# Hybrid mixer and top-4-of-32 MoE layer: turning the expert activations on ScalarE and VectorE instead of on TensorE

## The chip, the core and the metric

The kernel runs on one core of a Trainium2 chip. The metric is the device time of one execution in microseconds (us), as the median of repeated runs. A profile of one execution stands beside it: it has the start and the length of every instruction on TensorE (PE, with its weight loads as PEld), VectorE (DVE), ScalarE (ACT), GpSimd (POOL) and SyncE (SP), and of the DMA packets.

## What is computed

One layer over 1024 latent tokens of width 1024 (with 256 context tokens): a mixer of a recurrence (RG-LRU) and gated linear attention, layer norm, then a mixture of experts. Each token goes to 4 of 32 experts. The part that the change touches is the expert block:

```
def expert_block(args):
    tok, e = args
    xb = xt[tok]                                    # up to 128 rows of one expert
    gate = jnp.minimum(xb @ w_gate[e] + b_gate[e], SWIGLU_LIMIT)
    up = jnp.clip(xb @ w_up[e] + b_up[e], -SWIGLU_LIMIT, SWIGLU_LIMIT)
    act = (up + 1.0) * gate * jax.nn.sigmoid(SWIGLU_ALPHA * gate)
    return act @ w_down[e] + b_down[e]
```

All three weight matrices are 1024 x 1024 in fp32. The product with `w_down` needs `act` with its features on the partitions, while `gate` and `up` leave it with its rows on the partitions. So every block of `act` has to be turned between the two.

## The kernel before

After the mixer (to about 700 us) the kernel builds a table of jobs on the chip. A job is up to 128 rows of one expert, and its **kind** is 4 (full: 128 rows), 3 (96 rows), 2 (64) or 1 (32). A remainder of an expert is a job of kind 1 to 3, and its full jobs follow it. Jobs of kind 2 put the two halves of the 1024 output columns on the two halves of the partitions, jobs of kind 1 the four quarters on the four quarters, and kind 3 does both one after the other (`JOB_KINDS`). All engines walk the same table in loops of their own; branches (`by_kind`) pick the code for a kind.

TensorE's loop for job u works in this order: the first half of `gate_up` of job u (k = 0 to 3 of the eight 128-row blocks of `w_gate` and `w_up`), `turn` of job u-1 (transposes of `ub` by the identity into `psT`), the second half of `gate_up` of job u, `down` of job u-1. I write G(u) and D(u) for `gate_up` and `down` of job u.

VectorE's loop for job u: copy half of the turned activations of job u-1 from PSUM to `aT` (L1792), `turn_rows_in` for job u+1 (L1618, after G(u)), `swiglu` of job u (L1626 to L1641: bias of gate and of up, clamp, two products), `weigh` of job u-1 (L1607, L1612, after D(u-1)). The next `gate_up` waits for `gu_free`, which L1629 raises. ScalarE copies the other half of `aT` (L1217) and does the sigmoid (L1220). GpSimd gathers rows, spreads biases and scatters results.

Weights come in pieces of 1 MB into twelve fixed places: eight for gate and up (two for each pair of k), four for down. SP issues a piece of the next expert (L503, L531) when TensorE has raised `gu_used` or `dn_used` for that place, which it does in the last job of an expert. In `gate_up` the rise comes with the last sweep over k:

```
if k % 2 and sweep == sweeps[-1]:
    mm.then_inc(gu_used, 1)
```

Kind 3 has two sweeps, "half" and then "quarter", and each call of `gate_up` does both over its own range k0 to k1.

In the profiled execution there are 49 jobs. Jobs 2, 7, 11, 16, 21, 23, 30 and 31 are of kind 3; jobs 3, 5, 10, 12, 17, 18, 24, 32, 43 and 45 of kind 2; jobs 8, 15, 20, 27, 33, 35, 39 and 47 of kind 1; the other 23 of kind 4. Every job of kind 3 is the only one of its expert.

Of the kernel before, what the change touches and what calls it, by code (L numbers as in the profile page):

```python
# [13 lines left out]
ALU = mybir.AluOpType  # L14
# [23 lines left out]
def layer(nc, x, c, ctx, c_ctx, w_ada, b_ada, w_in, conv_w, conv_b, lru_wa, lru_ba, lru_wx, lru_bx,  # L38
# [41 lines left out]
    with ctxs:  # L80
# [159 lines left out]
        aT = reg(o, KD, P); o += 1024  # L240
        yb = reg(o, D); o += 1024
# [71 lines left out]
        act_turned, aT_act, aT_dve = sem("act_turned"), sem("aT_act"), sem("aT_dve")  # L313
# [98 lines left out]
        def natural(ap):  # L412
            return ap.rearrange("p (b a i) -> p b a i", a=4, b=KD)

# [10 lines left out]
        def _(sp):  # L425
# [193 lines left out]
        def down(pe, kind, u, order_):  # L619
            pe.wait_ge(aT_act, u + 1)  # L620
            pe.wait_ge(aT_dve, u + 1)
            pe.wait_ge(y_biased, u + 1)
            sweeps = {4: ("full",), 3: ("half", "quarter"), 2: ("half",), 1: ("quarter",)}[kind]
            for sweep in sweeps:
                for k in range(KD):
# [9 lines left out]
                    if sweep == "half":  # L635
                        for j in range(2):
                            mm = pe.matmul(ps[6][HT * j:HT * j + HT, :], aT[:, k % 4, HT * (k // 4):HT * (k // 4) + HT],  # L637
                                           w[:, j * BANK:(j + 1) * BANK],
                                           start=(k == 0), stop=(k == KD - 1), skip_group_check=True)
                    if sweep == "quarter":  # L640
                        for j in range(4):
                            mm = pe.matmul(ps[7][QR * j:QR * j + QR, 0:QW], aT[:, 4 + k % 2, QR * (k // 2):QR * (k // 2) + QR],  # L642
                                           w[:, j * QW:(j + 1) * QW],
                                           start=(k == 0), stop=(k == KD - 1), skip_group_check=True)
# [26 lines left out]

        def turn(pe, src, n, first=0):
            for k in range(first, n):
                mm = pe.transpose(psT[:, k * P:(k + 1) * P], src[:, k * P:(k + 1) * P], ident[:, :])  # L674
            return mm

        @block.tensor
        def _(pe):
# [297 lines left out]
            pe.nop().then_inc(act_turned, 1)  # L976
# [9 lines left out]
            with pe.Fori(0, OUTER) as o4:  # L986
                with pe.If(typ_of(pe, typ_p) + typ_of(pe, typ_c) > 0):
                    with pe.Fori(0, INNER) as i4:
                        u = o4 * INNER + i4 + 1
                        with pe.If(typ_of(pe, typ_p) + typ_of(pe, typ_c) > 0):  # L990
                            t, on_ = typ_of(pe, typ_c), ord_of(pe, ord_c, wait_c)
                            by_kind(pe, t, lambda kind: gate_up(pe, kind, u, on_, 0, KD // 2))
                            tp, op_ = typ_of(pe, typ_p), ord_of(pe, ord_p, wait_p)
                            with pe.If(tp > 0):
                                pe.wait_ge(act_ready, u + 1)
                                by_kind(pe, tp, lambda kind: turn(pe, ub, JOB_KINDS[kind][2] // P, JOB_KINDS[kind][1] // P).then_inc(act_turned, 1))
                                pe.nop()
                            by_kind(pe, t, lambda kind: gate_up(pe, kind, u, on_, KD // 2, KD))
# [24 lines left out]
        def _(act):  # L1023
# [182 lines left out]
            act.nop().then_inc(aT_act, 1)  # L1206
# [52 lines left out]
        def _(dve):  # L1259
# [360 lines left out]
            def swiglu(u, kind):  # L1620
# [7 lines left out]
                for p0, p1, c, b, n in parts:  # L1628
# [12 lines left out]
                dve.scalar_tensor_tensor(out=ub[:, w], in0=sg[:, w], scalar=s7, in1=ub[:, w], op0=ALU.min,  # L1641
                                         op1=ALU.mult).then_inc(act_ready, 1)
# [63 lines left out]
            dve.nop().then_inc(aT_dve, 1)  # L1706
# [307 lines left out]
```

## Time and profile before

| | us |
|---|---|
| time, median of 3 runs | 2355.92 (2355.53 to 2364.61) |
| span of the profiled execution, first to last instruction | 2352.5 |
| PE busy | 2191.9 (93% of the span) |
| DVE busy | 1021.4 |
| ACT busy | 466.7 |
| POOL busy | 444.8 |
| read from HBM | 480.51 MB, 218 GB/s over the span |

The profile has no other time for the profiled execution than its span; the median lies 3.4 us above it. A row of a group of instructions gives engine, line, operation, tiles, shapes, count, busy time and mean length, then the idle time of the engine just before it and what ended that. A row of the timeline gives the start, the length of a run of alike instructions, and in brackets the idle time before it. One fp32 matmul shows as two records, one transpose as one.

### The profile page before, as it was taken

What the parts mean: (1) busy time and instruction counts of PE and PEld (TensorE: products, weight loads), DVE (VectorE), ACT (ScalarE), POOL (GpSimd) and SP (SyncE); (2) the same over time, 40 slices, a digit from 0 to 9 for tenths busy, and PEclk for the clock granted to TensorE, in tenths of its full rate; (3) what the DMA queues carried; (4) which work ended last, traced back from release to release, by engine and by line L of the source; (5) the groups of instructions that cost most, each with busy time, mean ns of one, the idle gap of its engine ahead of it and who ended that gap; (6) DMA issues with size and microseconds to landing.
All of it is one profiled execution on the core that took longest, in us unless ns stands there. A gap on an engine that the chain in (4) does not pass through costs nothing.

```text
span 2352.5 us, 33568 instructions
## 1 busy us (share of the span) xinstructions
PE 2191.9 (93%) x9959; PEld 1018.7 (43%) x9960; DVE 1021.4 (43%) x1587; ACT 466.7 (20%) x624; POOL 444.8 (19%) x417
## 2 busy tenths in 40 slices
PE   5889999879968999999999899999999999999995
PEld 3444444464544444443443344444443444444442
DVE  3575754465775243444334243423253333222235
ACT  2334434331220111111111111111111111111113
POOL 0010100001231122222222132312213222122110
PEclk9989999889968999999999999999999999999997
DMA  8222221012252776889489999747899558897644
GB/s 330 84 67 69 89 72 36 1 73 84 89 214 91 240 296 213 298 291 400 135 284 399 355 354 407 256 158 246 297 376 349 204 174 297 291 324 240 214 128 154
DMA packets 168969, 510.55 MB, mean 217 GB/s; under 512 B 16434, under 2 KB 51002, under 8 KB 167770
## 3 DMA queue, kind: packets, MB, share of 16 engines
q1 hardware_dynamic: 153802, 474.25, 53.9%
q0 software_dynamic: 15120, 35.67, 6.9%
q8 instruction: 30, 0.49, 0.1%
q14 instruction: 17, 0.14, 0.0%
HBM read 480.51 MB, written 31.46 MB: 218 GB/s over the span
## 4 chain that ended last, share of the span: by engine, by line
PE 85%; DVE 7%; DMA 3%; issue 2%; ACT 1%; SPq 1%; DVEq 0%; POOL 0%; POOLq 0%
PE psall L605 27%; PE psall L633 14%; PE psall L609 10%; PE psall L776 10%; PE psall L637 5%; PE psall L614 4%; PE psall L764 3%; PE psall L887 2%; PE psall L881 2%; DMA arena<-in_w_down_dram 2%; PE psall L674 1%; PE psall L743 1%; DMA arena<-in_x_dram 1%; PE psall L642 1%; DVE arena L1423 1%
## 5 line engine op out<-in xcount | busy, mean ns | idle before, releaser
L605 PE MATMUL psall<-arena 128*128 128x512 f32 x1472 | 645.7, 597 | 27.5 <-issue 22.3
L605 PEld LDWEIGHTS psall<-arena 128*128 128x128 f32 x1472 | 278.6, 191 | 373.0 <-issue 373.0
L633 PE MATMUL psall<-arena 128*128 128x512 f32 x736 | 323.5, 598 | 4.8 <-DVE arena L1792 3.2
L609 PE MATMUL psall<-arena 128*64 128x512 f32 x1152 | 258.5, 600 | 8.9 <-DVE arena L1629 3.7
L1618 DVE STREAM_TRANSPOSE arena<-arena 128x1024 f32<-128x1024 f32 x49 | 61.0, 1246 | 453.6 <-PE psall L605 276.5
L776 PE MATMUL psall<-arena 128*128 128x512 f32 (+1 forms) x608 | 246.5, 563 | 0.7 <-ACT arena L1037 0.7
L633 PEld LDWEIGHTS psall<-arena 128*128 128x128 f32 x736 | 139.5, 191 | 183.3 <-issue 183.3
L1217 ACT COPY arena<-psall 128x512 f32<-128x512 f32 x49 | 28.7, 586 | 792.1 <-PE psall L674 792.1
L1792 DVE COPY arena<-psall 128x512 f32<-128x512 f32 x49 | 33.9, 692 | 323.3 <-PE psall L674 323.1
L776 PEld LDWEIGHTS psall<-arena 128*128 128x128 f32 x608 | 116.5, 192 | 120.6 <-issue 116.3
L1220 ACT ACTIVATE arena<-arena 128x1024 f32<-128x1024 f32 x49 | 51.8, 1057 | 582.5 <-DVE arena L1626 582.5
L1607 DVE TENSOR_TENSOR arena<-psall,arena 32x256 f32<-32x256 f32 (+2 forms) x123 | 79.8, 649 | 191.8 <-PE psall L633 147.7
L1893 POOL DMA_INDIRECT arena<-h_rows,lruw x144 | 147.0, 1021 | 83.0 <-POOL lruw L1886 39.4
L609 PEld LDWEIGHTS psall<-arena 128*64 128x64 f32 x1152 | 83.7, 138 | 167.4 <-issue 167.4
L637 PE MATMUL psall<-arena 128*64 128x512 f32 x576 | 128.6, 595 | 8.0 <-DMA arena<-in_w_down_dram 7.4
L1886 POOL COPY lruw<-arena 128x4 int32 (+1 forms) x48 | 9.2, 191 | 631.0 <-DVE arena L1618 602.5
L614 PE MATMUL psall<-arena 128*32 128x256 f32 x2048 | 117.3, 381 | 2.5 <-issue 1.4
L1907 POOL DMA_INDIRECT stream_rows<-arena,lruw x57 | 92.9, 1630 | 93.9 <-DMA stream_rows<-arena,lruw 42.2
L1612 DVE SCALAR_TENSOR_TENSOR arena<-arena,lruw,adarow 32x256 f32<-32x256 f32 (+2 forms) x123 | 90.9, 739 | 6.7
L614 PEld LDWEIGHTS psall<-arena 128*32 128x32 f32 x2048 | 64.1, 110 | 60.3 <-issue 22.9
L1626 DVE TENSOR_TENSOR arena<-psall,arena 32x256 f32<-32x256 f32 (+2 forms) x123 | 78.0, 634 | 14.0 <-PE psall L605 13.0
L637 PEld LDWEIGHTS psall<-arena 128*64 128x64 f32 x576 | 41.6, 137 | 91.6 <-issue 91.6
(319 smaller groups left out, 2098.6 us busy)
## 6 DMA issues: line engine op xcount, KB each, us to landing
arena<-in_w_gate_dram SPq DMA_DIRECT2D x128, 1024.0 KB, 6.5
arena<-in_w_up_dram SPq DMA_DIRECT2D x128, 1024.0 KB, 8.6
arena<-in_w_down_dram SPq DMA_DIRECT2D x128, 1024.0 KB, 8.9
arena<-in_w_ada_dram SPq DMA_DIRECT2D x16, 1024.0 KB, 5.3
arena<-in_w_ada_dram SPq DMA_DIRECT2D x4, 2048.0 KB, 14.2
arena<-in_w_in_dram SPq DMA_DIRECT2D x16, 512.0 KB, 4.0
arena<-in_x_dram SPq DMA_DIRECT2D x2, 2048.0 KB, 28.4
arena<-in_w_out_dram SPq DMA_DIRECT2D x1, 4096.0 KB, 14.1
```

What stands on the lines that cost most here:

```text
L605: mm = pe.matmul(ps[2 * g + s], xT[:, k, :], w[:, s * BANK:(s + 1) * BANK], start=(k == 0), stop=(k == KD - 1))
L609: mm = pe.matmul(ps[2 * g][HT * j:HT * j + HT, :], xT[:, k, 0:HT], w[:, j * BANK:(j + 1) * BANK], start=(k == 0), stop=(k == KD - 1), skip ...
L614: mm = pe.matmul(ps[2 * g + 1][QR * j:QR * j + QR, 0:QW], xT[:, k, r], w[:, j * QW:(j + 1) * QW], start=(k == 0), stop=(k == KD - 1), skip ...
L633: mm = pe.matmul(ps[6 + s], aT[:, k, :], w[:, s * BANK:(s + 1) * BANK], start=(k == 0), stop=(k == KD - 1))
L637: mm = pe.matmul(ps[6][HT * j:HT * j + HT, :], aT[:, k % 4, HT * (k // 4):HT * (k // 4) + HT], w[:, j * BANK:(j + 1) * BANK], start=(k == ...
L764: mm = pe.matmul(ps[i % JB][:, :], uT[:, k, j * P:(j + 1) * P], wv[:, k, :], start=(k == 0), stop=(k == KD - 1))
L776: mm = pe.matmul(ps[i % JB][0:w, 0:seg[1] - seg[0]], wring[n % WRING][:, k, 0:w], uT[:, k, seg[0]:seg[1]], start=(k == 0), stop=(k == KD - 1))
L1607: mm = dve.tensor_tensor(yb[p0:p1, c:c + n], psY[p0:p1, c:c + n], ebias[p0:p1, 2, b:b + n], ALU.add)
L1612: mm = dve.scalar_tensor_tensor(out=yb[p0:p1, c:c + n], in0=yb[p0:p1, c:c + n], scalar=(wcolq if c else wcol)[p0:p1], in1=adarow[p0:p1, 3, ...
L1626: mm = dve.tensor_tensor(gb[p0:p1, c:c + n], psG[p0:p1, c:c + n], ebias[p0:p1, 0, b:b + n], ALU.add)
L1893: pool.indirect_dma_start(out=xg[:, CW * t:CW * (t + 1)], out_offset=None, in_=h2_dram.rearrange("a (j n) -> (a j) n", n=CW), in_offset=ba ...
L1907: return pool.indirect_dma_start(out=to, out_offset=bass.IndirectOffsetOnAxis(ap=index, axis=0), in_=yb[:, cols], in_offset=None, bounds_c ...
```

## The change

TensorE no longer turns the activations. `gate_up` of a job now runs over all eight k in one call, and `down` of the job before follows at once. The last product of `swiglu` leaves the activations in `ub` (kinds 4, 2, and the first part of kind 3) or, reordered, in a new tile `act_rows` (kind 1 and the second part of kind 3). ScalarE then copies quarters (32 partitions x 256 columns) from `ub` to other partitions of `act_rows`: 16 copies for kind 4, 8 for kinds 3 and 2, none for kind 1. Each reads every eighth column and writes without gaps. VectorE turns 32 x 32 blocks from `act_rows` to `aT` in one instruction, and `down` waits for that. Since the features now lie on the partitions in another order (eight neighbours on one partition), `w_down` is loaded so that partition p gets rows 8p to 8p+7; a piece is two of these eight rows (8 KB in one run on each partition) where it was two separate rows of 4 KB.

```
             def dn_pieces(e, u):
                 for q in range(DNP):
                     sp.wait_ge(dn_used, DNP * u + (q + 1))
-                    w_v = w_down[0].rearrange("e (q c p) n -> e q p c n", c=2, p=P)[:, q]
+                    w_v = w_down[0].rearrange("e (p k) n -> e p k n", k=KD)[:, :, 2 * q:2 * q + 2]
...
         def down(pe, kind, u, order_):
-            pe.wait_ge(aT_act, u + 1)
-            pe.wait_ge(aT_dve, u + 1)
+            pe.wait_ge(aT_ready, u + 1)
...
-                            by_kind(pe, t, lambda kind: gate_up(pe, kind, u, on_, 0, KD // 2))
+                            by_kind(pe, t, lambda kind: gate_up(pe, kind, u, on_, 0, KD))
                             tp, op_ = typ_of(pe, typ_p), ord_of(pe, ord_p, wait_p)
-                            with pe.If(tp > 0):
-                                pe.wait_ge(act_ready, u + 1)
-                                by_kind(pe, tp, lambda kind: turn(pe, ub, JOB_KINDS[kind][2] // P, JOB_KINDS[kind][1] // P).then_inc(act_turned, 1))
-                                pe.nop()
-                            by_kind(pe, t, lambda kind: gate_up(pe, kind, u, on_, KD // 2, KD))
...
+            def spread(u, kind):
+                act.wait_ge(act_ready, u + 1)
+                if kind == 1:
+                    act.nop().then_inc(act_spread, 1)
+                    return
+                if kind == 4:
+                    moves = [(t, a, QW * a) for t in range(4) for a in range(4)]
+                else:
+                    moves = [(t, 2 * j + h, QW * h) for t in range(2) for j in range(2) for h in range(2)]
+                for t, a, c in moves:
+                    of = QR * t + (0 if kind == 4 else HT * (a // 2))
+                    mm = act.copy(by_block(act_rows[QR * a:QR * a + QR, QW * t:QW * t + QW]),
+                                  by_feature(ub[of:of + QR, c:c + QW]))
+                mm.then_inc(act_spread, 1)
...
-                            act.wait_ge(act_turned, u + 1)
-                            act.copy(aT[:, 0:4].rearrange("p k n -> p (k n)"), ps[4]).then_inc(aT_act, 1)
+                            by_kind(act, typ_of(act, typ_p), lambda kind: spread(u, kind))
...
+            def turn_act(kind):
+                lo, hi = JOB_KINDS[kind][1] // QW, JOB_KINDS[kind][2] // QW
+                dve.transpose(aT.rearrange("p b (t s) -> p t b s", t=4)[:, lo:hi],
+                              act_rows.rearrange("p (t b i) -> p t b i", t=4, b=KD)[:, lo:hi]).then_inc(aT_ready, 1)
...
-                            dve.wait_ge(act_turned, u + 1)
-                            dve.tensor_copy(aT[:, 4:8].rearrange("p k n -> p (k n)"), ps[5]).then_inc(aT_dve, 1)
+                            dve.wait_ge(act_spread, u)
+                            by_kind(dve, tp, turn_act)
```

TensorE, body of the job loop, the branches for kinds 4 and 3. Before, `gate_up` stands in two halves with the transposes (L674) between them:

```order
L605 MATMUL psall<-arena 128x512 x16
L650 UNCONDITIONAL_BRANCH
L591 ISA
L609 MATMUL psall<-arena 64x512 x16
L614 MATMUL psall<-arena 32x256 x32
...
L674 MATMUL psall<-ident,arena 128x128 x8
L650 UNCONDITIONAL_BRANCH
L674 MATMUL psall<-ident,arena 128x128 x6
...
L609 MATMUL psall<-arena 64x512 x16
L614 MATMUL psall<-arena 32x256 x32
```

After, L612, L616 and L621 are the same matmuls:

```order
L612 MATMUL psall<-arena 128x512 x32
L655 UNCONDITIONAL_BRANCH
L598 ISA
L616 MATMUL psall<-arena 64x512 x32
L621 MATMUL psall<-arena 32x256 x64
```

The transposes are gone, and in kind 3 all 64x512 matmuls (k = 0 to 7) now stand ahead of all 32x256 ones, where they took turns in two halves.

ScalarE, body of the job loop. Before, one copy from PSUM and the sigmoid:

```order
L1217 ACT_TABLE_LOAD
L1217 COPY arena<-psall 128x512
L1215 UNCONDITIONAL_BRANCH
L1218 COMPARE_AND_BRANCH
L1219 ISA
L1220 ACT_TABLE_LOAD
L1220 ACTIVATE arena<-arena 128x1024
```

After, the branches for kinds 4, 3 and 2, then the sigmoid (L1229):

```order
L1212 COPY arena<-arena 32x256 x16
L655 UNCONDITIONAL_BRANCH
L1202 ISA
L1212 ACT_TABLE_LOAD
L1212 COPY arena<-arena 32x256 x8
...
L1229 ACT_TABLE_LOAD
L1229 ACTIVATE arena<-arena 128x1024
```

One copy per job became 16 or 8, between the act of a job and the VectorE instruction that turns it.

## Rows read from the trace of the kernel before

**Rows 1.** The page's chain that ended last, share of the span by engine.

```profile
PE 85%; DVE 7%; DMA 3%; issue 2%; ACT 1%; SPq 1%; DVEq 0%; POOL 0%; POOLq 0%
```

**Rows 2.** Groups by shape: the transposes, and VectorE's block transpose of the next rows.

```profile
L674 PE MATMUL psall<-ident,arena 128*128 128x128 f32 x288 | 41.8, 282 | 2.5 <-DVE arena L1641 2.5
...
L1618 DVE STREAM_TRANSPOSE arena<-arena 128x1024 f32<-128x1024 f32 x49 | 61.0, 1246 | 453.6 <-PE psall L605 276.5 <-PE psall L614 99.2 <-PE psall L609 67.4
```

**Rows 3.** Timeline of TensorE, jobs 19 to 21: start, us, engine, line, [idle before].

```profile
1348.69 7.09 PE L637 MATMUL psall<-arena 128*64 128x512 f32 x32
1355.71 3.66 PE L614 MATMUL psall<-arena 128*32 128x256 f32 x64
1359.30 1.09 PE L674 MATMUL psall<-ident,arena 128*128 128x128 f32 x8
1360.32 3.66 PE L614 MATMUL psall<-arena 128*32 128x256 f32 x64
```

**Rows 4.** Timeline of VectorE in the same place.

```profile
1348.92 1.25 DVE L1618 STREAM_TRANSPOSE arena<-arena 128x1024 f32<-128x1024 f32 x1 [13.16 <-PE psall L605]
...
1354.65 1.23 DVE L1641 SCALAR_TENSOR_TENSOR arena<-arena 128x1024 f32<-128x1024 f32 x1
```

**Rows 5.** Timeline of TensorE, job 34 (full) between two quarter jobs.

```profile
1829.77 3.66 PE L642 MATMUL psall<-arena 128*32 128x256 f32 x64
1833.93 3.66 PE L614 MATMUL psall<-arena 128*32 128x256 f32 x64 [0.50 <-DVE arena L1629]
1837.53 1.09 PE L674 MATMUL psall<-ident,arena 128*128 128x128 f32 x8
1838.55 3.66 PE L614 MATMUL psall<-arena 128*32 128x256 f32 x64
1842.46 13.97 PE L633 MATMUL psall<-arena 128*128 128x512 f32 x32 [0.25 <-DVE arena L1792]
```

**Rows 6.** Groups by shape of ScalarE: immediate operands, strided and unstrided output, two partition starts.

```profile
L1062 ACT ACTIVATE arena<-arena 128x1280 f32<-128x1280 f32 x4 | 5.0, 1254 | 0.0
L1060 ACT ACTIVATE arena<-arena 128x1024 f32<-128x1024 f32 x4 | 4.2, 1040 | 0.0
L1109 ACT ACTIVATE arena<-psall,par 128x512 f32<-128x512 f32 x8 | 9.8, 1230 | 42.4 <-PE psall L776 42.4
L1109 ACT ACTIVATE arena<-psall,par 128x256 f32<-128x256 f32 x4 | 2.2, 562 | 4.9 <-PE psall L776 4.9
28.88 1.18 ACT L1031 COPY adarow<-psall 2x512 f32<-2x512 f32 x2 [17.67 <-PE psall L689]
```

**Rows 7.** Timeline of TensorE: a full job's half after a wait of 3.45 us.

```profile
1407.40 15.67 PE L605 MATMUL psall<-arena 128*128 128x512 f32 x32 [3.45 <-DVE arena L1629]
```

**Rows 8.** Timelines at the last job: VectorE's last product and TensorE.

```profile
2293.57 1.23 DVE L1641 SCALAR_TENSOR_TENSOR arena<-arena 128x1024 f32<-128x1024 f32 x1
...
2299.99 16.56 PE L633 MATMUL psall<-arena 128*128 128x512 f32 x32 [2.94 <-DVE arena L1792]
```

**Rows 9.** Timelines at job 30 (kind 3): TensorE, and SP's first issues.

```profile
1685.42 7.09 PE L609 MATMUL psall<-arena 128*64 128x512 f32 x32
...
1692.44 3.66 PE L614 MATMUL psall<-arena 128*32 128x256 f32 x64
...
1694.15 0.40 SPq L503 DMA_DIRECT2D arena<-in_w_gate_dram  x1
```

**Rows 10.** Stretches: us, busy of PE, PEld, DVE, ACT, POOL, clock, DMA share, GB/s.

```profile
18.00:34.00 16.00, 8.15 (x49) 2.68 (x42) 1.38 (x2) 1.15 (x2) 0.00 (x0) 0.83 1.01 413
1212.00:1320.00 108.00, 96.29 (x661) 38.78 (x652) 45.62 (x76) 16.83 (x16) 29.31 (x29) 0.97 1.02 389
1685.00:1802.00 117.00, 110.61 (x859) 45.84 (x858) 56.36 (x90) 16.83 (x16) 28.62 (x28) 1.00 0.95 356
```

**Rows 11.** Timeline of TensorE: the last waits for weights in the two stretches.

```profile
1318.72 1.94 PE L637 MATMUL psall<-arena 128*64 128x512 f32 x8 [1.87 <-DMA arena<-in_w_down_dram]
...
1800.02 1.94 PE L637 MATMUL psall<-arena 128*64 128x512 f32 x8 [1.03 <-DMA arena<-in_w_down_dram]
```

More of the change, by code:

```diff
@@ L240, in layer @@
         aT = reg(o, KD, P); o += 1024
+        act_rows = reg(O_X1 + 19456, D)
         yb = reg(o, D); o += 1024
@@ L312, in layer @@
             sem("g_biased"), sem("sg_ready"), sem("u_clipped"), sem("ug_ready"), sem("act_ready"))
-        act_turned, aT_act, aT_dve = sem("act_turned"), sem("aT_act"), sem("aT_dve")
+        act_spread, aT_ready = sem("act_spread"), sem("aT_ready")
         y_dve, y_stored, yq_stored, yb_free = sem("y_dve"), sem("y_stored"), sem("yq_stored"), sem("yb_free")
@@ L413, in natural, with by_feature, by_block @@
             return ap.rearrange("p (b a i) -> p b a i", a=4, b=KD)
+        def by_feature(ap):
+            return ap.rearrange("p (i b) -> p b i", b=KD)
+        def by_block(ap):
+            return ap.rearrange("p (b i) -> p b i", b=KD)
         def o_at(T, h):
@@ L636, in down @@
                         for j in range(2):
-                            mm = pe.matmul(ps[6][HT * j:HT * j + HT, :], aT[:, k % 4, HT * (k // 4):HT * (k // 4) + HT],
-                                           w[:, j * BANK:(j + 1) * BANK],
+                            mm = pe.matmul(ps[6][HT * j:HT * j + HT, :], aT[:, k, 0:HT], w[:, j * BANK:(j + 1) * BANK],
                                            start=(k == 0), stop=(k == KD - 1), skip_group_check=True)
@@ L641, in down @@
                         for j in range(4):
-                            mm = pe.matmul(ps[7][QR * j:QR * j + QR, 0:QW], aT[:, 4 + k % 2, QR * (k // 2):QR * (k // 2) + QR],
+                            mm = pe.matmul(ps[7][QR * j:QR * j + QR, 0:QW], aT[:, k, HT:HT + QR],
                                            w[:, j * QW:(j + 1) * QW],
@@ L670, in ord_of @@
             return eng.snap(bounded, min_val=16, max_val=16 * NE)
[L672 to L675, printed above, removed]
         @block.tensor
@@ L974, in job_lists @@
                 mm.then_inc(half_mm, 1)
-            pe.nop().then_inc(act_turned, 1)
             pe.wait_ge(tab_ready, 16)
@@ L1215, in _ @@
                         with act.If(typ_of(act, typ_p) > 0):
-                            act.wait_ge(act_turned, u + 1)
-                            act.copy(aT[:, 0:4].rearrange("p k n -> p (k n)"), ps[4]).then_inc(aT_act, 1)
+                            by_kind(act, typ_of(act, typ_p), lambda kind: spread(u, kind))
+                            act.nop()
                         with act.If(typ_of(act, typ_c) > 0):
@@ L1640, in swiglu @@
                 dve.wait_ge(ug_ready, u + 1)
-                dve.scalar_tensor_tensor(out=ub[:, w], in0=sg[:, w], scalar=s7, in1=ub[:, w], op0=ALU.min,
-                                         op1=ALU.mult).then_inc(act_ready, 1)
+                for p0, p1, c, b, n in parts:
+                    if p0 == 0:
+                        w = slice(c, c + n)
+                        out, in0, in1 = ub[:, w], sg[:, w], ub[:, w]
+                        if c:
+                            out, in0, in1 = by_block(act_rows[:, w]), by_feature(in0), by_feature(in1)
+                        mm = dve.scalar_tensor_tensor(out=out, in0=in0, scalar=s7, in1=in1, op0=ALU.min, op1=ALU.mult)
+                mm.then_inc(act_ready, 1)
+            def turn_act(kind):
+                lo, hi = JOB_KINDS[kind][1] // QW, JOB_KINDS[kind][2] // QW
+                dve.transpose(aT.rearrange("p b (t s) -> p t b s", t=4)[:, lo:hi],
+                              act_rows.rearrange("p (t b i) -> p t b i", t=4, b=KD)[:, lo:hi]).then_inc(aT_ready, 1)
             first_ranks(NT - 1, NT + 1)
@@ L1705, in _ @@
             turn_rows_in()
-            dve.nop().then_inc(aT_dve, 1)
+            dve.nop().then_inc(aT_ready, 1)
             dve.nop().then_inc(act_ready, 1)
```

2 lines of the change are left out of this document (1 added, 1 removed).

## The prediction

> **What bounds the kernel now.** I read the chain of waits first: 85% of the span hangs on PE [rows 1], so time goes away only where PE has less to do or waits less. Then the groups by shape, for the price of what goes and of its nearest kin [rows 2, 6], and the timeline of PE through the jobs [rows 3, 5]. There the matmuls of one job follow those of the next without a gap almost everywhere. The transposes (L674) lie in this row of work, so they cost their own time, and nothing waits for them but VectorE's and ScalarE's copies. Two stretches are different: from 1212 to 1320 us and from 1685 to 1802 us the DMA engines are busy at a share of 1.02 and 0.95 [rows 10], and each ends with PE waiting for weights [rows 11]. In these the bytes set the time, and not PE.
>
> **What goes from PE.** 288 transposes [rows 2]. Eight of them take from 1359.30 to 1360.32, 1.02 us until the next matmul starts [rows 3]; next to full jobs it is 0.88, and the sum over the 48 groups that lie between matmuls is 34.7 us. The last group is no part of it: there PE is idle anyway. VectorE's copy of 128x512 goes too, but it lies beside PE's work. First term: **-34.7 us**.
>
> **What the new chain costs.** From the end of G(u) to D(u) PE has D(u-1) and G(u+1) to do. In that time VectorE must turn the next rows and do the five steps of `swiglu`, ScalarE must make its copies, VectorE must turn blocks. At a full job the last product ends 7.2 us after G's end (1348.69 to 1354.65 + 1.23) [rows 3, 4]. The block transpose of a full job has the shape of L1618: 1.25 us [rows 2]; I add 0.1 us at either side of ScalarE's part. The copies are the unknown. On ScalarE 256 more columns cost 1254 - 1040 = 214 ns, so 256 columns with immediate operands cost 1040 - 3 x 214 = 398 ns [rows 6]. That is without a stride. L1109 with a gap-free output takes 562 ns for 256 columns, hence 348 + 214; into strided columns it takes 1230 ns for 512, hence 348 + 882, or 1.72 ns a column where 0.84 is normal. Our copies read with a stride of eight columns. No row shows a strided read from SBUF on this engine, so the bounds are 398 ns and 184 + 441 = 625 ns. I take 625, since L1109 is the only row of this engine with a stride. Do successive copies overlap? The two L1031 copies start on different partitions, and take 1.18 us for 2 x 575 ns: no overlap, 0.03 us between [rows 6]. Each copy here goes to another quarter than the one before. So a full job's 16 copies cost 16 x 0.655 = 10.5 us, or 16 x 0.43 = 6.9 at the lower bound, and aT is ready 7.2 + 0.1 + 10.5 + 0.1 + 1.25 = 19.1 us after G(u)'s end, or 15.5.
>
> Where is PE there sooner? Among full jobs, PE is away 42 us, and with a quarter job behind and a full one before, 21; all covered. The tight ones are these. Job 34 (full) stands between two quarter jobs: G(35) starts 4.16 us after G(34)'s end and takes 2 x 3.6, so PE is free at 11.4 [rows 5]. It waits 7.7 where 0.25 stands now, and after such a wait it restarts slowly: 3.45 us of idleness came before a half that took 15.67 us [rows 7] where 13.97 is usual [rows 5], 1.7 more. Together +9.2. Jobs 19 and 46 (half before, quarter behind): PE is free at 7.0 + 3.6 + 3.6 = 14.2 [rows 3], waits 4.9 and restarts slowly: 2 x 6.6 = +13.2. Job 9 (quarter before, half behind): free at 18.0, +1.1. Job 48 is the last, nothing covers it: its product ends at 2294.80, aT at 2306.7, against a start of D at 2299.99 [rows 8]: +6.8. Second term: 9.2 + 13.2 + 1.1 + 6.8 = **+30.3 us**. With the lower bound it is 5.6 + 2.6 + 0 + 3.2 = +11.4.
>
> The steps of narrow jobs have half the copies (5.2 us) or none. A job of kind 3 has its last product 12.3 us after G's end and would be ready at about 19; PE comes at 21 or later.
>
> **What the weights cost.** In kind 3 the old order did the half sweep over k = 0 to 3, then the quarter sweep over them, and released four places after 7.02 + 3.66 us: SP's first issue comes 8.7 us after G(30)'s start [rows 9]. Now the half sweep runs over all eight k (14.0 us) before the first quarter matmul, so the first release comes at 14.0 + 1.8 = 15.9 us. Where the DMA engines have nothing left to do at that time, 7.2 us are lost to them. That is so at job 30, since its four places were empty until then. The chain of bytes from there to 1800.02 is 36 pieces. It starts 7.2 us later, gets back some 1 us of its own gaps and, by the packets of 8 KB, 12 down pieces x 0.08 = 1.0 us (413 GB/s in a stretch of 8 KB packets [rows 10] against 400 in the middle of the first stretch), and has another gap of 0.4 at job 31: +5.7 us. The four groups of transposes in it (3.2 us) bring nothing. So this stretch is 8.9 us worse than the first term says. In the first stretch pieces queue at job 16 until about the new release; its chain stays whole, gains 1.2, and 2.9 us of transposes bring nothing: +1.7. Behind jobs 7 and 11 a narrow job follows, and the down pieces queue behind eight pieces of gate and up: 15.9 + 12 x 2.8 = 49.5 us for the last, where D(7) wants it at 21.4 + 14.0 + 7.3 + 3 x 1.8 = 48.1. I take +3.5 for both. Third term: 8.9 + 1.7 + 3.5 = **+14.1 us**.
>
> **The sum.** -34.7 + 30.3 + 14.1 = +9.7 us. The span goes from 2352.5 to 2362.2, and with the 3.4 us by which the median lies above the span, the time is **2366 us**. Its own range is 2355 to 2377: the slow restarts are uncertain by 4 us, the weights by 6.
>
> A page that speaks against this change: the Trainium skill, "SBUF — State Buffer", section "Door 1: The DMA port swizzle", says that accesses which cross to a new 16-byte line each time pay a penalty, so that fp32 may stride over four elements for free. Our copies stride over eight. By that rule the upper price stands; without it the sum would be 18.9 us lower. L1109's row agrees for a write; none here shows the read.
>
> **Rivals.** *Cheap copies.* A read with a stride is free, as nothing shows that it isn't. The second term is 11.4: -34.7 + 11.4 + 14.1 = -9.2, so 2347 us, range 2338 to 2353. For it: in ScalarE's strided row only the output is strided. Against: the output's store and the input's read go to the same memory. *Down pieces that come slowly.* The new view of `w_down` takes 8 KB from each 32 KB, over the whole 4 MB, where a piece was 1 MB in one run. If such a piece took twice its time (2.7 us more), the 12 pieces of each stretch bound by bytes would add 32 us, and 12 more in the jobs 7 and 11: 2366 + 76 = 2442 us. It decides from about 0.5 us a piece, which would bring 12 + 3 us. Against: the first loads take 8 KB from every 24 KB, and run at 413 GB/s [rows 10]. The Trainium skill, "DMA: Bandwidth & Descriptors", section "Latency and other measured facts", has large powers of two as a row pitch slow, but starts at 512 KiB with 207 GB/s of 214; by it 32 KB costs nothing. *The release doesn't matter.* If the queue at job 30 hides the late release, the third term is 5 and the time 2357, or with cheap copies 2338.
>
> **Chances.** The forecast 0.48, cheap copies 0.32, slow down pieces 0.08, no effect of the release 0.12 (half of it with cheap copies). A measurement of this kernel can tell 0.5% (11.8 us: below 2344.1, above 2367.7) from no change. Of the forecast 0.22 lies above 2367.7, the rest within; of cheap copies 0.15 lies below 2344.1; of the last rival 0.06 does. So faster 0.21, same 0.49, slower 0.30. The range from 2338 to 2380 leaves out the slow pieces and the tails, some 0.15.
>
> **What would show it.** The changed kernel's profile should have 23 x 16 + 18 x 8 = 512 copies of 32x256 on ScalarE at a mean of 625 ns (398 if a strided read is free); no idle time before D but at jobs 34, 19, 46, 9 and 48, put down to VectorE's block transpose; SP's first issue in job 30 some 16 us after its G starts; waits for `w_up` and `w_down` in jobs 32 and 33 that sum to some 12 us where 4 stand now; and packets of 8 KB for `w_down` at twice the time of those of 4 KB. The forecast is wrong if the copies overlap after all, if PE doesn't slow down after waits of 5 us, or if the first sweep of kind 3 isn't what holds the places.

## The result, and the profile after

The changed kernel takes 2373.7 us (median of its runs, 2371.5 to 2376.75), the kernel before beside it 2359.0. The ratio is 1.0061, with a 95% interval of 1.004 to 1.0081. That is 14 us slower, 9 to 19 by the interval; the forecast was 10 us slower and a time of 2366 us. The span is 2369.8 us, 17.3 longer. The page of the kernel after has busy times and the chain of waits [rows 1]:

```profile
PE 2163.5 (91%) x9671; PEld 1001.1 (42%) x9672; DVE 1040.2 (44%) x1595; ACT 762.5 (32%) x1079; POOL 445.8 (19%) x417
...
PE 79%; DVE 8%; DMA 5%; ACT 3%; issue 2%; SPq 2%; DVEq 0%; POOL 0%; ACTq 0%; POOLq 0%
```

PE is busy for 28.4 us less (2191.9 before), and the span still grew: its share of the chain fell from 85 to 79%, ScalarE and the DMAs got two points each, and VectorE and SP one each. The groups by shape say what the new operations cost [rows 2, 6]:

```profile
L1212 ACT COPY arena<-arena 32x256 f32<-32x256 f32 x512 | 334.4, 653 | 99.2 <-DVE arena L1656 86.9 <-issue 6.8
...
L1661 DVE STREAM_TRANSPOSE arena<-arena 128x1024 f32<-128x1024 f32 x23 | 28.6, 1245 | 109.0 <-ACT arena L1212 108.8 <-issue 0.2
```

A copy takes 653 ns (forecast 625), and nearly all the idle time of VectorE ahead of its block transpose ends with the last copy. The timeline of PE shows where it waits for this transpose, in jobs 9, 19, 34, 46 and 48 [rows 5, 7, 8]; line L639 is L633 of before:

```profile
1065.41 14.00 PE L639 MATMUL psall<-arena 128*128 128x512 f32 x32 [1.62 <-DVE arena L1661]
...
1369.98 15.48 PE L639 MATMUL psall<-arena 128*128 128x512 f32 x32 [5.48 <-DVE arena L1661]
...
1852.60 16.51 PE L639 MATMUL psall<-arena 128*128 128x512 f32 x32 [5.18 <-DVE arena L1661]
...
2255.42 16.48 PE L639 MATMUL psall<-arena 128*128 128x512 f32 x32 [4.96 <-DVE arena L1661]
...
2317.29 16.27 PE L639 MATMUL psall<-arena 128*128 128x512 f32 x32 [14.32 <-DVE arena L1661]
```

These are the five places that the prediction named, and no other `down` waits for the block transpose: the view of waits has `PE psall L639 <- DVE arena L1661` five times, 31.6 us in all. The same timeline shows two losses of another kind, ahead of the first `down` and inside `down` of job 7:

```profile
787.82 13.97 PE L639 MATMUL psall<-arena 128*128 128x512 f32 x32 [2.98 <-issue]
...
1001.64 1.94 PE L643 MATMUL psall<-arena 128*64 128x512 f32 x8 [1.10 <-DMA arena<-in_w_down_dram]
1004.26 1.94 PE L643 MATMUL psall<-arena 128*64 128x512 f32 x8 [0.68 <-DMA arena<-in_w_down_dram]
1008.65 1.94 PE L643 MATMUL psall<-arena 128*64 128x512 f32 x8 [2.46 <-DMA arena<-in_w_down_dram]
1011.87 1.94 PE L643 MATMUL psall<-arena 128*64 128x512 f32 x8 [1.28 <-DMA arena<-in_w_down_dram]
```

In SP's timeline the first issue of job 30 comes 15.6 us after G(30)'s start (1684.98 in PE's timeline), where it was 8.7 [rows 9]:

```profile
1700.58 0.41 SPq L510 DMA_DIRECT2D arena<-in_w_gate_dram  x1
```

To put the difference into places I take every start from the first `gate_up` (711.14 us before, 710.66 after), since the part ahead of it varies by some us between executions. From there to the end it is 1641.4 us before and 1659.1 after, 17.7 more. As in the forecast's sum, the transposes stand in the last row wherever they lay, also beside a named job; only the two stretches stand with what their transposes bring:

| place | forecast, us | measured, us |
|---|---|---|
| ahead of D(0): the wait of 2.98, and 0.7 before G(1) | 0 | +3.6 |
| jobs 7 and 11, `down` waits for its weights | +3.5 | +10.3 (6.2 and 4.0) |
| job 9 | +1.1 | +1.5 |
| jobs 19 and 46 | +13.2 | +14.6 (6.9 and 7.7) |
| job 34 | +9.2 | +10.4 |
| last job | +6.8 | +6.9 |
| first stretch bound by bytes (G(15) to G(19)) | -1.2 | -1.3 |
| second (G(30) to G(34)) | +5.7 | +4.0 |
| everything else, mainly transposes | -28.6 | -32.1 |

The figure of job 34 has a part that is no wait for the turn. G(35), which PE runs just before D(34), takes 2.9 us longer than before; it has four gaps of 0.3 us, put down to "issue", and slower matmuls around them:

```profile
1837.26 1.89 PE L621 MATMUL psall<-arena 128*32 128x256 f32 x26 [0.53 <-DVE arena L1638]
...
1841.65 5.77 PE L621 MATMUL psall<-arena 128*32 128x256 f32 x98 [0.34 <-issue]
```

It costs nothing here: D(34) waits for the turn anyway, and in the first experiment below, where G(35) is 2.0 us quicker, it waits 2.0 us longer. Some of the other kernels have this slow G(35) too (those with one transpose and with kind 3's order alone), others don't; its cause stays open.

### The profile page after: what moved, and what is told of

Same layout as the page of the kernel before. It is cut to its first block, busy times and chain, and to the rows that moved or that the text cites. A ratio compares the mean times of both kernels' runs of the same rounds, so it can differ in the third digit from the quotient of the medians.

```text
span 2369.8 us, 33439 instructions
## 1 busy us (share of the span) xinstructions
PE 2163.5 (91%) x9671; PEld 1001.1 (42%) x9672; DVE 1040.2 (44%) x1595; ACT 762.5 (32%) x1079; POOL 445.8 (19%) x417
## 4 chain that ended last, share of the span: by engine, by line
PE 79%; DVE 8%; DMA 5%; ACT 3%; issue 2%; SPq 2%; DVEq 0%; POOL 0%; ACTq 0%; POOLq 0%
PE psall L612 26%; PE psall L639 14%; PE psall L776 10%; PE psall L616 9%; DMA arena<-in_w_down_dram 4%; PE psall L643 3%; PE psall L621 3%; PE psall L764 3%; PE psall L887 2%; PE psall L881 2%; ACT arena L1212 2%; PE psall L743 1%; DMA arena<-in_x_dram 1%; PE psall L647 1%; DVE arena L1432 1%
## 5 line engine op out<-in xcount | busy, mean ns | idle before, releaser
L612 PE MATMUL psall<-arena 128*128 128x512 f32 x1472 | 641.7, 596 | 27.9 <-issue 23.5
L612 PEld LDWEIGHTS psall<-arena 128*128 128x128 f32 x1472 | 280.3, 191 | 383.6 <-issue 383.6
L1212 ACT COPY arena<-arena 32x256 f32<-32x256 f32 x512 | 334.4, 653 | 99.2 <-DVE arena L1656 86.9
L1229 ACT ACTIVATE arena<-arena 128x1024 f32<-128x1024 f32 x49 | 51.8, 1057 | 968.4 <-DVE arena L1635 876.8
L639 PE MATMUL psall<-arena 128*128 128x512 f32 x736 | 329.9, 607 | 35.1 <-DVE arena L1661 31.6
L616 PE MATMUL psall<-arena 128*64 128x512 f32 x1152 | 253.5, 597 | 9.8 <-DMA arena<-in_w_up_dram 4.5
L639 PEld LDWEIGHTS psall<-arena 128*128 128x128 f32 x736 | 141.9, 195 | 217.9 <-issue 183.6
L616 PEld LDWEIGHTS psall<-arena 128*64 128x64 f32 x1152 | 86.6, 137 | 173.1 <-issue 173.0
L643 PE MATMUL psall<-arena 128*64 128x512 f32 x576 | 131.1, 597 | 16.9 <-DMA arena<-in_w_down_dram 16.0
L621 PE MATMUL psall<-arena 128*32 128x256 f32 x2048 | 118.8, 383 | 10.6 <-DMA arena<-in_w_up_dram 4.6
L1661 DVE STREAM_TRANSPOSE arena<-arena 128x1024 f32<-128x1024 f32 (+3 forms) x49 | 47.2, 962 | 128.0 <-ACT arena L1212 120.5
L621 PEld LDWEIGHTS psall<-arena 128*32 128x32 f32 x2048 | 70.4, 110 | 63.0 <-issue 27.9
L1621 DVE SCALAR_TENSOR_TENSOR arena<-arena,lruw,adarow 32x256 f32<-32x256 f32 (+2 forms) x123 | 89.6, 728 | 6.7
## 6 DMA issues: line engine op xcount, KB each, us to landing
arena<-in_w_out_dram SPq DMA_DIRECT2D x1, 4096.0 KB, 13.9
```

The costliest lines, as they stand in the source:

```text
L612: mm = pe.matmul(ps[2 * g + s], xT[:, k, :], w[:, s * BANK:(s + 1) * BANK], start=(k == 0), stop=(k == KD - 1))
L616: mm = pe.matmul(ps[2 * g][HT * j:HT * j + HT, :], xT[:, k, 0:HT], w[:, j * BANK:(j + 1) * BANK], start=(k == 0), stop=(k == KD - 1), skip ...
L621: mm = pe.matmul(ps[2 * g + 1][QR * j:QR * j + QR, 0:QW], xT[:, k, r], w[:, j * QW:(j + 1) * QW], start=(k == 0), stop=(k == KD - 1), skip ...
L639: mm = pe.matmul(ps[6 + s], aT[:, k, :], w[:, s * BANK:(s + 1) * BANK], start=(k == 0), stop=(k == KD - 1))
L643: mm = pe.matmul(ps[6][HT * j:HT * j + HT, :], aT[:, k, 0:HT], w[:, j * BANK:(j + 1) * BANK], start=(k == 0), stop=(k == KD - 1), skip_gro ...
L1212: mm = act.copy(by_block(act_rows[QR * a:QR * a + QR, QW * t:QW * t + QW]), by_feature(ub[of:of + QR, c:c + QW]))
```

## Experiments

All figures "from the first `gate_up`" are of one profiled execution of each kernel, like those above. Between executions they vary: D(0) alone took 13.9 us to the next start in two kernels with the new order and 15.3 to 15.6 in the others. The ratios are to the kernel before, on the same chip.

**Kind 3 in two half sweeps.** The changed kernel, but `gate_up` of kind 3 again does both sweeps over k = 0 to 3 and then both over 4 to 7.

```
-            for sweep in sweeps:
+            cuts = (k0, (k0 + k1) // 2, k1) if kind == 3 and k1 - k0 == KD else (k0, k1)
+            for sweep, k0, k1 in [(s, a, b) for a, b in zip(cuts, cuts[1:]) for s in sweeps]:
                 for k in range(k0, k1):
```

> The changed kernel, but gate_up of a job of kind 3 does its two sweeps over k = 0 to 3 and then over k = 4 to 7, as before the change. Theory (late release of the weight places in kind 3 costs time): SP's first issue in a kind 3 job comes 9 us after its start and not 15.6; the waits for w_down in D(7) and D(11), 5.5 and 3.3 us, are gone; the stretch of jobs 30 to 33 gets 4 to 6 us shorter; in all 10 to 14 us less than the changed kernel's span of 2369.8, so 2356 to 2360. Rival (the new view of w_down makes its pieces come late): the waits stay, and the span is within 2 us of 2369.8.

Measured: 2359.05 us, ratio 1.0023 (1.0012 to 1.0033); from the first `gate_up` 13.0 us less than the changed kernel. SP's first issue in job 30 comes 8.7 us after its start again (15.6 in the changed kernel), D(11) has no wait for weights, and neither has D(7):

```profile
1007.13 7.09 PE L644 MATMUL psall<-arena 128*64 128x512 f32 x32 [0.23 <-issue]
```

So the order of the sweeps, and not the removal of the transposes or the new view, is what made the weights late. At job 34 nothing is gained: G(35) is 2.0 us quicker, and the wait grows by as much, from 5.2 to 7.2.

**That order alone, in the kernel before.** The transposes stay; only kind 3 runs over all eight k ahead of them.

```
-by_kind(pe, t, lambda kind: gate_up(pe, kind, u, on_, 0, KD // 2))
+by_kind(pe, t, lambda kind: gate_up(pe, kind, u, on_, 0, KD if kind == 3 else KD // 2))
...
-by_kind(pe, t, lambda kind: gate_up(pe, kind, u, on_, KD // 2, KD))
+by_kind(pe, t, lambda kind: gate_up(pe, kind, u, on_, KD // 2, KD) if kind != 3 else pe.nop())
```

> The kernel before, transposes and all, with one thing changed: in jobs of kind 3 gate_up runs over all eight k ahead of the transposes of the job before, so that the quarter sweep (and with it the release of the places of gate and up) comes after the whole half sweep. Its third effect: turned activations of the job before come 10.7 us later, for which PE waits nowhere. Theory (the late release costs time by itself): jobs 7 and 11 wait for down pieces, 5 to 9 us together, jobs 32 and 33 wait 5 us more, so 10 to 14 us more than before. Rival (in the changed kernel the weights come late for another reason): within 3 us of before.

Measured: 2371.66 us, ratio 1.0052 (1.0032 to 1.0072), 14.3 us more from the first `gate_up`. Of this 3.1 lie at job 7, 1.0 at job 11 and 5.2 in the second stretch up to G(35), and another 3.0 in G(35), which I had not expected. Nor had I expected what the edit does besides: the turned activations come later, and PE does wait for them, in `down` of jobs 1, 6, 10, 22, 29 and 30, for 0.9 to 1.5 us each:

```profile
1102.37 7.09 PE L637 MATMUL psall<-arena 128*64 128x512 f32 x32 [1.45 <-DVE arena L1792]
```

They add 3.2 us of the 14.3. So the late weights by themselves cost 9 us (12 with G(35)), and that the whole comes out near the 13.0 of the repair is partly chance. Jobs 7 and 11 show why the changed kernel loses more there. From the start of G(7) to that of G(9), which follows D(7), it is 56.0 us before and 54.1 with the two half sweeps, but 59.5 here and 60.1 in the changed kernel. From G(11) to G(13) the four are 55.8, 54.2, 57.8 and 58.1. So with the late release the end of `down` is set by its last piece of weights, and what the missing transposes save ahead of it only makes the wait longer.

**The new view of `w_down` undone.** The changed kernel with `w_down` loaded as before. Its rows then don't match the order of the features, so its output is not the reference's.

```
-w_v = w_down[0].rearrange("e (p k) n -> e p k n", k=KD)[:, :, 2 * q:2 * q + 2]
+w_v = w_down[0].rearrange("e (q c p) n -> e q p c n", c=2, p=P)[:, q]
```

> The changed kernel, but w_down is loaded by the old view (two separate rows of 4 KB on each partition); since the activations are in the new order, this kernel multiplies each activation with another row of w_down, at the same cost. Theory (release order): the same waits in D(7) and D(11), span within 2 us of 2369.8, at most 2 us more in the two stretches bound by bytes (12 pieces x 0.08 us each). Rival (the view is slow): the waits in D(7) and D(11) go, and 9 us or more are gained.

Measured: 2377.74 us, ratio 1.0091 (1.0075 to 1.0107), 6.9 us *more* than the changed kernel from the first `gate_up`. The rival of slow down pieces is out: without the new view nothing is gained, and the waits in D(7) are still there (5.1 us). But only a small part of the 6.9 us is shown to be the view's. In each of the two stretches bound by bytes it is 0.7 us, within what I had allowed. Another 2.5 us lie ahead of G(2), before and in D(0), and 2.3 in D(7), where matmuls run slowly behind a wait (16 of them take 3.65 us at the usual pace):

```profile
790.39 15.67 PE L639 MATMUL psall<-arena 128*128 128x512 f32 x32 [3.96 <-issue]
...
1013.71 6.63 PE L643 MATMUL psall<-arena 128*64 128x512 f32 x16 [3.23 <-DMA arena<-in_w_down_dram]
```

The loss ahead of G(2) is no sign of the view: five kernels below that have the new view lose 2.0 to 3.4 us in the same place. Of the last 0.8 us 0.7 are again slow matmuls, in D(19).

**Packed reads.** The changed kernel, but VectorE's last product writes its result by blocks (it reads and writes with a stride instead), so ScalarE's copies read runs of 32 columns. The number of copies stays.

```
-                        out, in0, in1 = ub[:, w], sg[:, w], ub[:, w]
-                        if c:
-                            out, in0, in1 = by_block(act_rows[:, w]), by_feature(in0), by_feature(in1)
+                        out, in0, in1 = by_block((act_rows if c else gb)[:, w]), by_feature(sg[:, w]), by_feature(ub[:, w])
...
-                                  by_feature(ub[of:of + QR, c:c + QW]))
+                                  by_block(gb[of:of + QR, 0:D if kind == 4 else BANK])[:, :, c // KD:(c + QW) // KD])
```

> The changed kernel, but VectorE's last product reads every eighth column and writes gb without gaps, by blocks, and ScalarE's copies read runs of 32 neighbouring columns. Theory (ScalarE's price is the strided read): a copy takes some 400 ns where it takes 653, 16 of them 6.9 us where they take 10.6; the product of a full job takes 2.2 us where it takes 1.23 (its 256-column form with a stride takes 669 ns, without 439), so aT comes 2.7 us sooner. Waits in D(34), D(19), D(46) fall from 5.2 to 2.5, the last job gains 2.7, some 13 us in all with restarts: span 2355 to 2360. Rival (the price is that of 32 partitions, or of changing them): 653 ns stays, and the span grows by some 4 us.

Measured: 2358.02 us, ratio 1.0012 (1.0001 to 1.0023), 13.1 us less from the first `gate_up`. The groups by shape of this kernel:

```profile
L1212 ACT COPY arena<-arena 32x256 f32<-32x256 f32 x512 | 205.9, 402 | 124.8 <-DVE arena L1654 119.2
...
L1654 DVE SCALAR_TENSOR_TENSOR arena<-arena 128x1024 f32<-128x1024 f32 x23 | 46.6, 2027 | 2.4
```

A copy costs 402 ns now, which is the prediction's lower bound of 398. So the stride is the difference between the bounds. VectorE pays 0.8 us for it once (2027 ns for 1225), ScalarE had paid 0.25 us sixteen times. PE's waits fall to 2.22 us at job 19, 2.07 at job 46 and 11.22 at job 48. At job 34 the wait is 5.08, since G(35) is not slow here and PE comes 3.0 us sooner.

**Both repairs.**

> Both edits, those of kind 3's sweeps and of the packed product. If the two terms are independent, the gains add: 2369.8 - 12 - 13 = 2345, some 7 us (0.3%) less than the kernel before at 2352.5. If either rival holds, 2357 to 2372.

Measured: 2346.38 us, ratio 0.9958 (0.9943 to 0.9974), 25.9 us less than the changed kernel from the first `gate_up`. The two effects add up, 13.0 + 13.1, and with them the change becomes faster than the kernel before, by 0.4%.

**Only one copy.** The changed kernel with `for t, a, c in moves[:1]:` in `spread`.

> The changed kernel with only the first of ScalarE's copies in every job (the other quarters of act_rows stay stale, so this output isn't the reference's): aT is ready 9.8 us sooner after the last product of a full job, 4.6 us sooner in kinds 2 and 3. Theory (the row of copies costs its own length wherever PE is there sooner): the idle time before down of jobs 34, 19, 46 and 9 (5.2 + 5.5 + 5.0 + 1.6 us) goes but for a rest at job 34, the 14.3 us before the last down become 4.5, and the slow matmuls behind these waits (2.5 us at job 34, 1.5 at 19 and 2.5 at 46) come at their usual pace. 16.5 + 9.8 + about 4 = 30 us less than the changed kernel from the first gate_up on, of it 3 to 5 us given back in waits for weights, so 25 to 28 less. Rival (PE's waits are set elsewhere, by the other work of VectorE): under 12 us less.

Measured: 2345.31 us, ratio 0.9942 (0.9922 to 0.9963), 27.4 us less than the changed kernel from the first `gate_up`. The sum fits, but one part doesn't: the last `down` still waits 7.9 us, not 4.5. VectorE's timeline at the last job shows why:

```profile
2283.76 1.23 DVE L1656 SCALAR_TENSOR_TENSOR arena<-arena 128x1024 f32<-128x1024 f32 x1
2285.35 0.15 DVE L1610 COPY lruw<-lruw 128x1 f32 x1 [0.36 <-issue]
2285.57 1.72 DVE L1616 TENSOR_TENSOR arena<-psall,arena 32x256 f32<-32x256 f32 x4
2287.40 1.95 DVE L1621 SCALAR_TENSOR_TENSOR arena<-arena,lruw,adarow 32x256 f32<-32x256 f32 x4
2289.38 1.25 DVE L1661 STREAM_TRANSPOSE arena<-arena 128x1024 f32<-128x1024 f32 x1
```

The block transpose follows without a gap on `weigh` of job 47 (L1610 to L1621, 4 us). So there is a second chain under the copies: once they take less than some 4.4 us, VectorE's own queue holds the transpose.

**One transpose a job.** The kernel before with the first block of `turn` alone; 239 of the 288 transposes are left out, and the output is not the reference's.

> The kernel before with one transpose in each job where it has 8, 6, 4 or 2 (the other blocks of psT stay stale, so this output isn't the reference's): 239 of the 288 transposes are gone, in the same order of work. Theory (PE's row of matmuls is the bound outside of the two stretches bound by bytes): 239 x 0.12 = 29 us less, of which 5 us are absorbed in the two stretches: 23 to 26 us less than before. Rival (it is absorbed in much more of the program): under 15 us less.

Measured: 2337.49 us, ratio 0.9903 (0.9886 to 0.992), which is 19 to 27 us; from the first `gate_up` only 16.7. Seven transposes of a full job bring 0.77 us, and all that are left out between matmuls 22.1 (34.7 - 12.6), not the 29 that I had multiplied out. So 5.4 us are given back: 2.6 in G(35), some 1.4 in the first stretch bound by bytes, 0.8 in a wait for weights at job 11 and the rest in small parts. The transposes lie on the path, and what is absorbed is about the 5 us that I expected.

**Copies shared with VectorE.** Both repairs, and VectorE makes every second copy right after its last product.

```
+                if kind == 1:
+                    dve.nop().then_inc(dve_spread, 1)
+                else:
+                    dve.wait_ge(act_ready, u + 2)
+                    move(dve, kind, 1).then_inc(dve_spread, 1)
...
                             dve.wait_ge(act_spread, u)
+                            dve.wait_ge(dve_spread, u)
```

> The kernel with both repairs (packed reads, two half sweeps in kind 3), in which VectorE makes every second copy, right after its last product, and ScalarE the others. A full job has 8 copies on each engine, 3.3 us on ScalarE where 6.6 stood. Theory (the chain from the last product to aT is what PE waits for, and VectorE is free then): 3.3 us less at job 34 and at job 48, 1.6 less at each of jobs 19 and 46, some 2 us of slow restarts less: 10 to 12 us less than with both repairs alone. Rival (the copies of the two engines hold each other up, or VectorE's copies push its later steps): no gain, or slower.

Measured: 2348.41 us, ratio 0.9952 (0.9936 to 0.9967); from the first `gate_up` 2.3 us more than with both repairs alone. The rival holds. ScalarE is done after 3.3 us, but VectorE isn't. Its timeline at job 19:

```profile
1347.74 2.07 DVE L1659 SCALAR_TENSOR_TENSOR arena<-arena 128x1024 f32<-128x1024 f32 x1
1349.85 4.37 DVE L430 COPY arena<-arena 32x256 f32<-32x256 f32 x8
1354.25 0.15 DVE L1613 COPY lruw<-lruw 128x1 f32 x1
1354.33 1.39 DVE L1621 TENSOR_TENSOR arena<-psall,arena 64x512 f32<-64x512 f32 x2
1355.84 1.51 DVE L1626 SCALAR_TENSOR_TENSOR arena<-arena,lruw,adarow 64x512 f32<-64x512 f32 x2
1357.75 1.25 DVE L1669 STREAM_TRANSPOSE arena<-arena 128x1024 f32<-128x1024 f32 x1 [0.40 <-issue]
```

2.0 us of the copies' 4.37 are one copy beside a broadcast of GpSimd (last section). Copies and `weigh` stand one after the other ahead of the transpose, and PE's wait at job 19 grew from 2.23 to 3.21 us. By the ratios, which overlap, this kernel and the one with both repairs are equal; the sharing gains nothing.

**Another order on VectorE.** Both repairs and shared copies, but in a job VectorE now does: last product, bias of the job before, 6 of the 16 copies, block transpose, and only then the scaling of the job before.

```
-                        with dve.If(tp > 0):
-                            dve.wait_ge(act_spread, u)
-                            dve.wait_ge(dve_spread, u)
-                            settle(dve)
-                            by_kind(dve, tp, turn_act)
...
                             by_kind(dve, tp, lambda kind: weigh(u, kind, orderp))
+                        with dve.If(typ_of(dve, typ_c) > 0):
+                            by_kind(dve, typ_of(dve, typ_c), lambda kind: spread_dve(u, kind))
+                            dve.wait_ge(act_spread, u + 1)
+                            dve.wait_ge(dve_spread, u + 1)
+                            by_kind(dve, typ_of(dve, typ_c), turn_act)
+                        with dve.If(tp > 0):
+                            by_kind(dve, tp, lambda kind: scale_out(u, kind))
```

> The kernel with both repairs, with VectorE's work of a job in another order: last product, bias of the job before (3 of its 4 us in shared and one_copy stood ahead of the turn), 6 of 16 copies (ScalarE makes the other 10), turn of the blocks, and only then the scaling of the job before. Theory (what holds the turn in shared and one_copy is VectorE's own queue: copies and weigh stand between the last product and the turn): at a full job with a quarter job before it, the turn starts 4.1 us after the last product instead of 6.6, so the stall before down of jobs 34 and 48 is 2.7 us shorter than with both repairs alone, and that of jobs 19 and 46 goes: 7 to 9 us less than with both repairs alone, 0.993 of the kernel before. Rival (something else than this queue holds the turn): the same as both repairs alone, 0.996.

Measured: 2332.67 us, ratio 0.9894 (0.9875 to 0.9912), 14.6 us less than with both repairs alone from the first `gate_up`. This is the fastest kernel here, 1.1% faster than before. PE's rows at jobs 34, 46 and 48:

```profile
1827.52 14.00 PE L652 MATMUL psall<-arena 128*128 128x512 f32 x32 [1.25 <-DVE arena L1674]
...
2222.90 14.00 PE L652 MATMUL psall<-arena 128*128 128x512 f32 x32 [0.28 <-DVE arena L1674]
...
2276.79 16.61 PE L652 MATMUL psall<-arena 128*128 128x512 f32 x32 [8.84 <-DVE arena L1674]
```

The waits fell by about what was expected (3.1, 1.8 and 2.4 us; the one at job 19, 2.2 us, is gone). The gain is larger than the 7 to 9 us because the matmuls at four places are no longer slow: D(19), D(34) and D(46) take 13.8 to 13.9 us to the next start, where they took 15.3 to 15.6, and G(22) takes 27.70 where it took 29.29, behind a wait that hardly changed (3.24 us for 3.34). These four bring 6.5 us, which I had left out of the sum. The kernel differs from the one with both repairs in two things, the order and who makes the copies; the kernel with shared copies has the second alone (8 of 16 on VectorE), and gained nothing.

## Why the prediction was right, and where it was off

**What bounds the kernel** was read rightly: PE's row outside of the two stretches, bytes inside them. The kernel with one transpose shows both.

**The first term** (-34.7 us, -28.6 outside of the stretches) held, with 32.1 measured for everything that isn't named in the table. Most of the 3.5 us more lie at six places where a job of kind 3 or 1 follows a full job: there 1.3 to 1.7 us went, and the transposes had taken 1.02. The rest are small parts.

**The second term** (+30.3 us) had the right mechanism at the five places named, and came out at 1.5 + 14.6 + 10.4 + 6.9 = 33.4 us. The waits themselves are close: 5.5 and 5.0 at jobs 19 and 46 (forecast 4.9), and at job 34 5.2 beside a G(35) that is 2.9 us longer, together 8.1 (forecast 7.7). The slow matmuls behind them cost 1.5 to 2.5 us, and not 1.7. The choice that decided the term was the price of a copy. The row with a strided *output* was the only one of ScalarE with a stride, and it gave 625 ns for what turned out to be 653. That a strided read costs what a strided write does was a guess that came true. The unstrided bound, 398, is what packed reads cost, 402. ScalarE's timeline has the 16 copies of the last job as one run of 10.48 us, where 10.5 were forecast. The sentence on the 16-byte lines of the Trainium skill ("SBUF — State Buffer", section "Door 1: The DMA port swizzle") agrees with these two rows: the same copy with runs of 32 columns costs 402 ns, with a step of eight 653. Its limit of four columns was not tried. The rival of cheap copies, priced 18.9 us lower, falls with them. Packed reads took 13.1 off and not 18.9, since VectorE's product pays 0.8 us for them, since at job 34 PE comes sooner and waits as long as before, and since 3.4 us were lost ahead of G(2).

**The third term** (+14.1 us) had the right mechanism. SP's first issue in job 30 came at 15.6 us, forecast at some 16, and the repair of the order gives 13.0 us back. The first stretch came out at -1.3 us, as forecast, and the second at +4.0 for +5.7: the waits for `w_gate`, `w_up` and `w_down` in jobs 32 and 33 sum to 8 us, not 12. The packets of 8 KB of `w_down` took 315 ns on average in the first stretch and those of 4 KB 169 before, so less than twice.

Mis-sized was the step on jobs 7 and 11. The forecast had the last down piece at 49.5 us after the start of G(7), where D(7) wants it at 48.1, and took 3.5 us for both jobs; they cost 10.3. The time of wanting was right: with the two half sweeps D(7) starts at 42.6 us, and its last quarter 5.4 later. The time of arrival was not: D(7) got its last piece at 53.7 us (1011.87 against 958.17 in PE's timeline). SP's first issue came at 15.6, as forecast, so the twelve pieces took 38.2 us from there and not 12 x 2.8 = 33.6. Beside them GpSimd's queue moved 1.5 MB in these jobs, which the forecast had at nothing; whether that is the whole difference was not tried. At job 11 the last piece came at 51.8. With these two arrivals the forecast's own step gives 5.6 + 3.7 = 9.3 us.

**What the forecast had not at all** is the 2.98 us before the first `down`, put down to "issue". All the variants of the changed kernel have it (3.0 to 4.0 us), and neither the kernel with kind 3's order alone nor the one with one transpose has it. So it comes with the new order of code on PE, in which nothing stands between the end of the first `gate_up` pair and the first execution of `down`. The trace has a clue: the DMA queue of kind "instruction" moves a packet of 16 KB at 783.95 us, 0.9 us ahead of this wait, and in each of the other variants one begins 0.4 to 1.0 us ahead of it. That points to the loading of code. But the kernel before also has such a packet at its D(0) (785.37 for 785.62 us), without a wait, and no run isolates it, so the cause stays open.

The errors sum up to some 8 us: +3.6 ahead of D(0), +6.8 at jobs 7 and 11, +3.1 in the second term, -1.9 in the stretches, and -3.5 in the rest. So the time came out 8 us above the forecast, inside its own range of 2355 to 2377, in part because errors of both signs met. The measured 0.6% lies just above the 0.5% that was called no change; the forecast had given "slower" 0.30.

## What to carry to other kernels

Work taken off the bounding engine is worth its own length only where the chain that replaces it ends before that engine comes back, so list the places where it comes back soonest (narrow jobs, the last job) and sum the chain for these alone. When calls are merged, look at what else their order had decided: here the point at which buffers were released, which cost more than a third of the gain. And before a part of a chain is shortened, look for the engine's next queued work behind it; the last step came with moving 2 us of scaling behind the turn, after sharing the copies alone had gained nothing.

## What the runs showed of the hardware

**A wait of PE can cost more than its length.** In the changed kernel the granted clock after the wait of 5.18 us before D(34) is 0.50 for four us, the lower of the two levels (1.2 GHz), and back at 1.00 some 8 us later. The columns of this view of stretches are those of [rows 10]:

```profile
1853.00:1857.00 4.00, 4.00 (x5) 1.45 (x5) 3.75 (x7) 0.83 (x1) 1.20 (x2) 0.50 0.00 0
1857.00:1861.00 4.00, 4.00 (x10) 1.86 (x9) 2.42 (x7) 1.34 (x2) 2.85 (x3) 0.91 0.43 106
1861.00:1869.00 8.00, 8.00 (x20) 3.47 (x19) 0.00 (x0) 0.17 (x1) 0.00 (x0) 1.00 0.98 360
```

Behind waits of some 5 us `down` took 15.5 to 16.9 us, behind 1.62 us and less 14.00. Between these the length of the wait doesn't tell it. D(0) took 13.97 behind 2.98 us in the changed kernel and 15.67 behind 3.23 in the kernel with both repairs; D(46) took 14.00 behind 2.07 with packed reads and 15.70 behind 2.06 with both repairs. The same half of G(17) took 9.96 us behind 3.45 in the kernel before and 7.09 behind 3.46 in the one with one transpose:

```profile
1261.73 9.96 PE L609 MATMUL psall<-arena 128*64 128x512 f32 x32 [3.45 <-DVE arena L1629]
```

```profile
1253.74 7.09 PE L609 MATMUL psall<-arena 128*64 128x512 f32 x32 [3.46 <-DVE arena L1629]
```

So a wait that goes away can give back 1.5 to 2.5 us beside itself, and a difference of that size at one place between two single executions needs another row to show its cause.

**A copy of VectorE beside a broadcast of GpSimd ends with it.** The eight copies of 32x256 took 2.38 us at one full job and 4.37 at others. VectorE's and GpSimd's timelines in the kernel with shared copies:

```profile
1164.65 2.38 DVE L430 COPY arena<-arena 32x256 f32<-32x256 f32 x8
...
1199.18 4.38 DVE L430 COPY arena<-arena 32x256 f32<-32x256 f32 x8
```

```profile
1198.30 3.03 POOL L1966 PARTITION_BROADCAST arena<-adarow  x1 [0.44 <-issue]
```

The eight aren't all slower. The view of this line in the slow place (shortest, median and longest of the eight, in ns) has one long copy:

```profile
L430 DVE COPY arena<-arena x8: 282/286/2285, 1199.2 to 1203.3; 32x256 f32<-32x256 f32 x8
```

Of VectorE's 256 copies in this kernel 19 took over 1 us (1.3 to 2.4), and each of the 19 runs beside a `PARTITION_BROADCAST` and ends 0.14 to 0.15 us after it. In the kernel with the other order the 11 copies of over 400 ns do the same. No run takes the broadcast away, so this is an observation in 30 places and not an experiment. ScalarE's eight copies beside both took 3.30 us each time.

**A pitch of 32 KB costs the DMA nothing here.** Pieces in runs of 8 KB, one in every 32 KB, moved no slower than pieces of 1 MB in one run that go in packets of 4 KB: a packet of 8 KB took 315 ns, two of 4 KB 338, and each of the two stretches bound by bytes was 0.7 us shorter with the runs of 8 KB.
